# First attention of a two-block kernel: scores by three float32r products of high and low parts, two score tiles issued together in each second step, and the gate rows spilled to memory

## The reference, cut to what matters

```python
q = jnp.concatenate([q_nope, q_rope], axis=-1)
k = jnp.concatenate([k_nope, broadcast(k_rope)], axis=-1)      # k_rope is the same for all heads
scores = jnp.einsum("bqhd,bkhd->bhqk", q_b, k) * scale
mask = key_chunk[None, :] <= q_chunk[:, None]                  # chunks of 64 tokens
probs = jax.nn.softmax(jnp.where(mask, scores, -jnp.inf), axis=-1)
return jnp.einsum("bhqk,bkhd->bqhd", probs, v)
```

## Time and profile before

| | us |
|---|---|
| median of 3 runs | 2780.64 |
| lowest and highest | 2779.86, 2781.82 |
| the profiled execution, its own time | 2778.42 |
| its span in the trace | 2776.6 |
| TensorE busy in the span | 2643.3 (95%) |
| first score product of the attention | starts at 281.6 |
| first product of the delta rule behind it | starts at 466.71 |

### The profile page before, as it was taken

How to read it: one execution, slowest core, us unless ns; L and a number is a source line. 1 busy time by engine, 2 the same in 40 slices (tenths; PEclk the granted TensorE clock), 3 DMA queues, 4 the chain that set the end, 5 groups by cost and what they waited for, 6 DMA issues and landing times.

```text
span 2776.6 us, 39285 instructions
## 1 busy us (share of the span) xinstructions
PE 2643.3 (95%) x15530; PEld 2137.2 (77%) x15530; DVE 1879.3 (68%) x2265; ACT 1237.7 (45%) x2316; POOL 408.6 (15%) x354
## 2 busy tenths in 40 slices
PE   7999998999799999999999999899998999999997
PEld 6887566887688888888778888655677888888886
DVE  3466554664687777888974664489646655578889
ACT  3323565332777773333553333467316433343332
POOL 4322001347300000000300000001375000000002
PEclk9999999999999999999999999999999999999999
DMA  3210000004356664332323123411253232343333
GB/s 135 54 38 15 8 6 25 3 21 171 106 168 211 189 198 164 117 121 107 137 91 121 62 91 106 168 60 35 89 196 112 101 111 103 122 164 109 121 106 122
DMA packets 213489, 290.49 MB, mean 105 GB/s; under 512 B 16552, under 2 KB 143807, under 8 KB 213311
## 3 DMA queue, kind: packets, MB, share of 16 engines
q1 hardware_dynamic: 195918, 227.75, 24.8%
q10 hardware_dynamic: 17392, 60.30, 5.5%
HBM read 220.91 MB, written 67.11 MB: 104 GB/s over the span
## 4 chain that ended last, share of the span: by engine, by line
PE 78%; DVE 11%; ACT 4%; POOL 3%; issue 3%; DMA 1%; SPq 0%; ACTq 0%; DVEq 0%; POOLq 0%
PE ps L1739 7%; PE ps L1741 7%; PE ps L1740 7%; PE ps L1794 6%; PE ps L1796 6%; PE ps L1795 6%; PE ps L1877 4%; PE ps L1879 4%; PE ps L1878 4%; PE ps L1530 3%; PE ps L1436 2%; PE ps L1309 1%; PE ps L1311 1%; PE ps L1310 1%; PE ps L1676 1%
## 5 line engine op out<-in xcount | busy, mean ns | idle before, releaser
L1794 PE MATMUL ps<-down_t_hi,down_s_hi 128*128 128x512 f32 x896 | 349.4, 390 | 4.0 <-DVE acc L3332 2.2
L1796 PE MATMUL ps<-down_t_hi,down_s_lo 128*128 128x512 f32 x896 | 348.7, 389 | 0.0
L1795 PE MATMUL ps<-down_t_lo,down_s_hi 128*128 128x512 f32 x896 | 348.6, 389 | 0.0
L2492 ACT CAST down_s_hi<-down_a 128x2048 fp32r<-128x2048 f32 x56 | 107.2, 1915 | 368.7 <-PE ps L1796 327.1
L1142 POOL TENSOR_SCALAR mean_sq<-ssq 128x1 f32<-128x1 f32 x64 | 36.6, 571 | 1294.7 <-ACT squares_junk_ffn L2030 1244.6
L1739 PE MATMUL ps<-act_hi,up_hi 128*128 128x512 f32 (+1 forms) x544 | 205.7, 378 | 6.1 <-issue 2.8
L1740 PE MATMUL ps<-act_lo,up_hi 128*128 128x512 f32 (+1 forms) x544 | 204.9, 377 | 0.0
L1741 PE MATMUL ps<-act_hi,up_lo 128*128 128x512 f32 (+1 forms) x544 | 204.8, 376 | 0.0
L1794 PEld LDWEIGHTS ps<-down_t_hi,down_s_hi 128*128 128x128 f32 x896 | 168.2, 188 | 41.7 <-issue 7.4
L1796 PEld LDWEIGHTS ps<-down_t_hi,down_s_lo 128*128 128x128 f32 x896 | 168.2, 188 | 35.3
L1795 PEld LDWEIGHTS ps<-down_t_lo,down_s_hi 128*128 128x128 f32 x896 | 168.2, 188 | 34.6
(11 more groups left out here) (383 smaller groups left out, 6511.6 us busy)
## 6 DMA issues: line engine op xcount, KB each, us to landing
down_a<-hid_spill SPq DMA_DIRECT2D x32, 1024.0 KB, 6.6
hid_spill<-up_hid ACTq DMA_DIRECT2D x30, 1024.0 KB, 6.2
w_ada<-in_w_ada SPq DMA_DIRECT2D x48, 512.0 KB, 4.0
up_raw<-in_w_in SPq DMA_DIRECT2D x18, 1024.0 KB, 5.1
raw<-in_w_out SPq DMA_DIRECT2D x32, 512.0 KB, 3.7
up_raw<-in_w_up SPq DMA_DIRECT2D x16, 1024.0 KB, 5.6
down_b<-in_w_down SPq DMA_DIRECT2D x16, 1024.0 KB, 6.5
up_raw<-in_w_mlp_in SPq DMA_DIRECT2D x16, 1024.0 KB, 5.3
```

Source lines behind the costliest of these rows:

```text
L1794: pe.matmul(out, ops["s_hi"][:, k, cols], ops["t_hi"][:, k, :], start=first, stop=False, skip_group_check=True)
L1795: pe.matmul(out, ops["s_hi"][:, k, cols], ops["t_lo"][:, k, :], start=False, stop=False, skip_group_check=True)
L1796: mm = pe.matmul(out, ops["s_lo"][:, k, cols], ops["t_hi"][:, k, :], start=False, stop=last, skip_group_check=True)
```

## The change

In words, with the line numbers of the new kernel:

1. **Scores in parts.** `q_f` and `k_f` become `q_hi`, `q_lo`, `k_hi`, `k_lo` (float32r: a high part, and the rest as a low part). Each float32 score product becomes three float32r products (lines 1485 to 1487), and a piece of fewer than 256 keys is computed 256 wide.
2. **The parts have to be made.** ScalarE's `mla_take` now writes the high parts, and VectorE subtracts (`mla_low_part`, two instructions of 64x512 for each of n = 0, 1, 4, 5; line 2997). The rotated features go first to `rope_t`, then ScalarE makes their high part (`mla_rope_high`, two copies of 32x512 for each half) and VectorE the low one (`mla_rope_low`, two instructions; line 2986). For pair 0 and 1 the rotated key's parts are copied by ScalarE.
3. **A projection waits for the subtraction.** It may reuse its bank only when `mla_low_part` has read it: n = 2, 3 and 5 now wait for the low parts of n = 0, 1 and 4 (they waited for the copies).
4. **Two score tiles together.** TensorE's step s issues, when s is even, the scores of items s + 1 and s + 2; when s is odd, none.
5. **Order ahead of pair 0.** The projections of pair 0 stand in another order; the second rotation of pair 0, the last conv panel's product and the delta rule's scales move from before item 0 to after items 0, 1 and 10 of VectorE's list.
6. **Gate rows spilled.** The low parts lie where the gate rows were, so SP writes the eight gate tiles (256 KB each) to memory behind its last weight panel of that stage, the key rotation waits for it (`gate_out`), and SP reads them back after the scores of pair 2 (`gate_back`, for the delta rule). VectorE's eight gate multiplications by the norm's gain come behind the eight first instructions, not between them.

The lists of POOL are the same. The diff, cut to its core:

```diff
+            for t in range(NT):
+                sp.wait_ge(sem("gate_silu"), NT + t + 1)
+                sp.dma_start(gate_d[t], gate[:, t, :]).then_inc(sem("gate_out"), 16)
...
+            sp.wait_ge(sem("mla_scores"), SB_ITEMS * (MLA_PAIRS - 1))
+            for t in range(NT):
+                sp.dma_start(gate[:, t, :], gate_d[t]).then_inc(sem("gate_back"), 16)
...
                 if n == 0:
                     pe.wait_ge(sem("mla_w_in"), 160 * (i + 1))
-                if i and n in (2, 3):
-                    pe.wait_ge(sem("proj_read"), 8 * i + 2 * n - 1)
+                if i == 1 and n == 0:
+                    pe.wait_ge(sem("mla_feat_done"), MLA_FEAT_AT[0, "low", 1])
+                elif i == 1 and n == 1:
+                    pe.wait_ge(sem("mla_feat_done"), MLA_FEAT_AT[0, "sum", 1])
+                elif i and n in (2, 3):
+                    pe.wait_ge(sem("mla_feat_done"), MLA_FEAT_AT[i, "low", n - 2])
                 elif n == 4 and i > 1:
                     pe.wait_ge(sem("mla_o_done"), 2 * (i - 1) + 1)
                 elif i and n == 5:
-                    pe.wait_ge(sem("proj_read"), 8 * i + 7)
+                    pe.wait_ge(sem("mla_feat_done"), MLA_FEAT_AT[i, "low", 4])
...
                 pe.wait_ge(sem("mla_exp_done"), SB_ITEMS * i + s + 1)
                 for f in range((n + HALF - 1) // HALF):
-                    w = min(HALF, n - f * HALF)
-                    mm = pe.matmul(ps[:, 2 * h + f, 0:w], q_f[i % 2][h][0:DQK, t * P:(t + 1) * P],
-                                   k_f[i % 2][h][0:DQK, f * HALF:f * HALF + w], start=True, stop=True)
+                    w = max(min(HALF, n - f * HALF), 2 * P)
+                    q, k = slice(t * P, (t + 1) * P), slice(f * HALF, f * HALF + w)
+                    pe.matmul(ps[:, 2 * h + f, 0:w], q_hi[i % 2][h][0:DQK, q], k_hi[i % 2][h][0:DQK, k], start=True, stop=False)
+                    pe.matmul(ps[:, 2 * h + f, 0:w], q_hi[i % 2][h][0:DQK, q], k_lo[i % 2][h][0:DQK, k], start=False, stop=False)
+                    mm = pe.matmul(ps[:, 2 * h + f, 0:w], q_lo[i % 2][h][0:DQK, q], k_hi[i % 2][h][0:DQK, k], start=False, stop=True)
...
                 for s in range(SB_ITEMS):
-                    if s + 1 < SB_ITEMS:
+                    if s % 2 == 0:
                         mla_scores(i, s + 1)
-                    elif not last:
-                        mla_scores(i + 1, 0)
+                        if s + 2 < SB_ITEMS:
+                            mla_scores(i, s + 2)
+                        elif not last:
+                            mla_scores(i + 1, 0)
...
+            def mla_rope_high(i, n):
+                cols = slice(n * HALF, (n + 1) * HALF)
+                act.wait_ge(sem("mla_feat_done"), MLA_FEAT_AT[i, "sum", n])
+                for h in range(2):
+                    act.copy(q_hi[i % 2][h][rr, cols], rope_t[rr, h * HALF:(h + 1) * HALF]).then_inc(sem("rope_hi"), 1)
...
+                act.wait_ge(sem("mla_k_rope_done"), 1)
+                for h in range(2):
+                    act.copy(k_hi[0][h][rr, :], k_sum[rr, :]).then_inc(sem("rope_hi"), 1)
...
+            def mla_take(i, n):
+                cols = slice(n % 2 * HALF, (n % 2 + 1) * HALF)
+                act.wait_ge(sem("mla_proj"), mla_chunk_count(i, n))
+                for h in range(2):
+                    act.copy((q_hi if n < 2 else k_hi)[i % 2][h][0:NOPE, cols],
+                             ps[h * NOPE:(h + 1) * NOPE, MLA_BANKS[n] if i else MLA_FIRST_BANKS[n], :]).then_inc(sem("proj_read"), 1)
...
+                    if i == 0 and s == 2:
+                        mla_rope_high(0, 1)
+                    if s in (5, 7) and not last:
+                        mla_rope_high(i + 1, s // 2 - 2)
+                    if i == 0 and s == 10:
+                        mla_key_copy(0, k_hi, k_hi[0][0])
+                        mla_key_copy(1, k_hi, k_hi[0][0])
+                    if i == 0 and s == 12:
+                        mla_key_copy(0, k_lo, k_lo[0][0])
+                        mla_key_copy(1, k_lo, k_lo[0][0])
...
-            for n in (0, 1, 4, 5):
-                mla_take(0, n)
+            mla_take(0, 4)
+            mla_key_high()
+            mla_take(0, 1)
+            mla_rope_high(0, 0)
+            mla_take(0, 5)
...
-                dve.wait_ge(sem("gate_silu"), t + 1)
+            for t in range(NT):
+                dve.wait_ge(sem("gate_silu"), NT + t)
                 gh = gate[:, t, :].rearrange("p (h e) -> p h e", h=GDN_HEADS)
-                ch.link(dve.tensor_tensor(gh, gh, out_norm_row[:].unsqueeze(1).broadcast_to([P, GDN_HEADS, P]), ALU.mult))
+                dve.tensor_tensor(gh, gh, out_norm_row[:].unsqueeze(1).broadcast_to([P, GDN_HEADS, P]), ALU.mult)\
+                    .then_inc(sem("gate_silu"), 1)
+            dve.wait_ge(sem("gate_silu"), 2 * NT)
...
+                dve.wait_ge(sem("gate_out"), FROM["gate_out"] + 16 * NT)
...
+            def mla_rope_low(i, n):
+                cols = slice(n * HALF, (n + 1) * HALF)
+                dve.wait_ge(sem("rope_hi"), FROM["rope_hi"] + mla_rope_hi(i, n))
+                for h in range(2):
+                    ins = dve.tensor_tensor(q_lo[i % 2][h][rr, cols], rope_t[rr, h * HALF:(h + 1) * HALF],
+                                            q_hi[i % 2][h][rr, cols].bitcast(F32), ALU.subtract)
+                ins.then_inc(sem("mla_feat_done"), 1)
...
+            def mla_low_part(i, n):
+                cols = slice(n % 2 * HALF, (n % 2 + 1) * HALF)
+                hi, lo = (q_hi, q_lo) if n < 2 else (k_hi, k_lo)
+                dve.wait_ge(sem("proj_read"), mla_took(i, n))
+                for h in range(2):
+                    ins = dve.tensor_tensor(lo[i % 2][h][0:NOPE, cols], ps[h * NOPE:(h + 1) * NOPE, MLA_BANKS[n] if i else MLA_FIRST_BANKS[n], :],
+                                            hi[i % 2][h][0:NOPE, cols].bitcast(F32), ALU.subtract)
+                ins.then_inc(sem("mla_feat_done"), 1)
...
+                    if i == 0 and s == 0:
+                        mla_rotate(0, 1)
+                    if i == 0 and s == 1:
+                        conv_silu(GDN_PANELS - 1)
+                    if i == 0 and s == 2:
+                        mla_low_part(0, 5)
+                    if i == 0 and s == 3:
+                        mla_rope_low(0, 1)
+                    if i == 0 and s == 10:
+                        gdn_scales()
...
-                    if s - 1 in MLA_STEPS[2:4] and not last:
-                        mla_rotate(i + 1, MLA_STEPS.index(s - 1) - 2)
...
+                    if s in (2, 3) and not last:
+                        mla_low_part(i + 1, s - 2)
+                    if s == 4 and not last:
+                        mla_rotate(i + 1, 0)
+                    if s == 5 and not last:
+                        mla_rope_low(i + 1, 0)
+                    if s == 6 and not last:
+                        mla_rotate(i + 1, 1)
+                        mla_low_part(i + 1, 4)
+                    if s == 7 and not last:
+                        mla_rope_low(i + 1, 1)
+                    if s == 9 and not last:
+                        mla_low_part(i + 1, 5)
+            mla_rotate(0, 0)
+            mla_low_part(0, 0)
+            mla_low_part(0, 4)
+            key_low()
+            mla_rope_low(0, 0)
+            mla_low_part(0, 1)
```

144 lines of the change are left out of this document (84 added, 60 removed).

## The result

| | before | after |
|---|---|---|
| median of 4 runs each, us | 2781.23 | 2813.27 |
| lowest and highest | 2779.86, 2781.93 | 2812.07, 2814.38 |
| first score product to the delta rule's first product | 281.62 to 466.71 | 278.48 to 499.90 |
| length of the stage | 185.1 | 221.4 |

The ratio is 1.0117, with a 95% interval of 1.0101 to 1.0133: slower by 32 us. The forecast was 2818.

What follows compares the result with a forecast made beforehand. TensorE was taken to bound the kernel nearly everywhere. Products -9.4 and waits +47.3 gave +37.9; with -0.5 for the order, 2778.4 became 2815.8, and 2.2 more for the median 2818 us, range 2807 to 2828.

Steps and rivals of the forecast that it cites:

- Score products: TensorE's score products in the stage: three float32r products cost less than one float32 product, -9.4 us, bounds -12 to -6.
- the first pair's projections: Pair 0's projections wait behind work moved into VectorE's list and the low part of n = 0: +4.1 us.
- Two score tiles together: Last pair's loop takes 7.44 us, before 5.28; with the low parts TensorE's waits in the stage grow by 47.3.
- over 25 us: Sign in the new profile: TensorE's waits before line 1485, ended by ScalarE's exponentials, total over 25 us.
- Low parts: VectorE's subtractions between two maxima: a chain of 7.87 us until projection 5 may reuse its bank; TensorE gets there after 4.69.
- Projection 5: TensorE waits 3.18 us for VectorE's line 2997 in each of three pairs, where the wait was nought; +9.5 together.
- The clock: Rival 4: granted clock falls in the stage; some 2925 us if throughout, about 2828 or more for a tenth; 5%.
- Order ahead of pair 0: Before the stage: the scores of item 1 at 282.0 instead of 282.46; -0.5 us taken, with -1 to +3.
- Gate rows: SP's 2 MB of writes have 76 us until the key rotation and cost nothing; without that cover some 10 to 20 us.
- Hidden waits: Rival 1, in the stage: TensorE saves its products and no exponential is missed, -5.9 us, 2775; 3%.
- harmless grouping: Rival 3, in the stage: only the low parts cost, a turn behind a turn does not hold ScalarE; +11, 2792; 5%.
- only the grouping: Rival 2, in the stage: only the grouping costs, the low parts find gaps in VectorE's list; +24, 2804; 5%.

Runs made afterwards that it cites:

- the spread version: New kernel with one score tile in each step, projections 4 and 5 a step later and low parts moved by a step or two; 2785.6 us, ratio 1.0013.
- one product of three: New kernel with only the product of the two high parts, the two products with low parts left out; 2813.8 us, ratio 1.0118.

## Why the prediction was right, point by point

*Score products.* In the last pair's rows the products start 0.23 apart for 512 keys, 0.17 to 0.18 for 384 and 0.12 for 256 (472.18 to 474.37 of its timeline), as taken. But the first of each tile costs 0.1 more, for which the sum had no term: where TensorE waits for nothing, the loop saved 0.43 and not 0.58. The 9.4 were over-sized. What of them is left can be seen only with the grouping out of the way: the spread version has pairs 1 to 3 shorter than the old ones by 0.1, 0.1 and 1.6, and pair 0, which takes over VectorE's moved work and had 4 us at 1.2 GHz, longer by 7.2 (282.71 to 331.02). The forecast gave the first pair's projections 4.1 of new waits.

*Two score tiles together.* Forecast 0.90, 0.72, 1.34 of waiting in a loop of 7.44; measured 0.88, 0.41, 0.8 in 7.13. The mechanism is as described, and two experiments from opposite sides price it: +24.4 when added alone (replayed +28.6), -20.6 when taken back (replayed -26.6). Both came out 4 to 6 smaller. The sign "over 25 us" of waits for exponentials before line 1485 was not met: they are 15.7. The term was over-sized in the last two waits of the loop, because ScalarE's list was added up in durations, 4.41, where the distances between starts give 3.77; for TensorE the prediction had made that distinction, for ScalarE not.

*Low parts.* Projection 5 was given 3.18 in each of three pairs. Its rows show, as idle time until VectorE's line 2997, 2.73, 1.21 and 0.62. This term was over-sized in two pairs: in pairs 1 and 2 the wait for VectorE was ended a step earlier, before the scores of item 8, by the rotated low part (line 2986, 1.96 idle in each), and TensorE then reached projection 5 late, partly at 1.2 GHz. VectorE's chain of 7.8 us is as forecast (7.87). The first pair's wait before projection 2, forecast 3.19, has 2.87.

*The clock.* Here the prediction failed in one step, and by a sign that it had named itself ("if the granted clock drops"). It read "the trace, which shows none in this stage, speaks against it" and gave the lower clock 5%. It fell, in three of four pairs, for 23 us. That the time still came out near the forecast is luck in part: the waits were shorter than forecast by about what the clock took (half of the 23 us, as an estimate, if the list was full in them). The last pair, which had no fall, took 53.46 against 56 forecast; the third, with 10 us at 1.2 GHz, 56.77. The trace of before could have told, just behind the stage:

```profile
471.56 0.68 PE L1530 MATMUL ps<-consts,t_inv_T 64*64 64x64 f32 x16 [2.87 <-DVE t_inv_T L2988]
```

From 473.7 to 477.1 its granted clock is 0.50. The prediction looked at the stage alone, where the longest wait is 1.93 idle, and its own replay put waits of over 3 us into the new one. In the new kernel the falls stand behind waits of 1.96 to 2.87 us, in other runs also behind 1.40 to 1.83 and once, with the grouping alone, behind one of 0.73 (434.14), and not behind every one of these. The Trainium skill (TensorE: Matmul & The Clock Gate, "A second HAM failure mode: psum-queue depth-cycling") describes such a case for another kernel: TensorE idling briefly and often between groups of products lets the clock swing between its two rates, and the throughput suffers. The traces here agree: rows at 0.50 and 1.00 side by side, and 0.78 to 0.82 in the pairs with one product of three.

*Order ahead of pair 0, and what surrounds the stage.* The first score product was expected a little before its old place of 281.6 and came at 278.48. In the other kernels with the new order it came between 280.0 and 282.7, in four with the old order between 281.3 and 281.6, so one trace doesn't place it: most of the 3.1 us is what executions differ by ahead of the stage. Taking them off and adding 1.5 behind the stage, the span grew by 34.7, of which the stage is 36.3.

*Gate rows.* Nothing, as forecast; the key rotation starts at 265.25 in the new kernel, before 268.

*The rivals.* Hidden waits (2775) and harmless grouping (2792) are refuted by the two experiments on the grouping; "only the grouping" is nearest, but low parts and clock add 12 us to it (209.5 against 221.4), net of what the products save.

## What to carry to other kernels

When instructions are regrouped, write down for one loop what stands between each producer and its consumer before and after; a share of 45% on ScalarE hid that every exponential was wanted at once. Work that is cut from an engine which waits may bring nothing when more idling comes with the lower clock: the same two products were worth 16 us with one score tile in each step and nothing with two. Price a change that adds waits of 1.5 to 3 us with some time at 1.2 GHz, even if the trace before shows none in the stage: look through the whole trace for what stands behind waits of that length. Place added work on a second engine where that engine has gaps, step by step: low parts moved by a step or two gave 10 us here, the clock's part in it included.

## What the runs showed of the hardware

With two of three score products left out, the grouped kernel was as slow as with all (2813.8 and 2813.3 us), its stage 4.7 us longer in the one trace of each (226.1 against 221.4): 35 us less work, 67 us more at 1.2 GHz. And the same wait of 1.76 us, at the same place in two pairs of one kernel, had 6.8 us at 1.2 GHz behind it in one and none in the other. Waits of 1.40 us can have them too, and one of 1.93 in the old kernel had none.
